# A two-layer trunk in split fp32: sums of normed tokens taken from PSUM, and VectorE's order around the MLP's seven-product multiplications

## The reference

```python
h2 = _rmsnorm(x, norm2_g[l])
x = x + jnp.square(jax.nn.relu(h2 @ w_ff1[l])) @ w_ff2[l]
```

## Time and profile before

| | |
|---|---|
| runs | 2473.15, 2473.32, 2476.62 us; median 2473.32 |
| profiled execution | 2465.62 us, its span 2463.8 us |
| granted TensorE clock, mean | 0.954 of full speed |
| busy, share of the span | TensorE 91%, VectorE 60%, GpSimd 43%, ScalarE 35% |
| first MLP | from about 502 to 1226 us of the span |
| second MLP | from about 1728 us to the end |

### The profile page before, as it was taken

One profiled execution on the slowest core, in us unless ns is written; L12 is line 12 of the kernel. 1 busy time (PEld: TensorE's weight loads), 2 busy tenths in 40 slices (PEclk: granted clock), 3 DMA queues, 4 the chain that ended last, 5 costly groups with the idle time before them and its releaser, 6 DMA issues.

```text
span 2463.8 us, 36690 instructions
## 1 busy us (share of the span) xinstructions
PE 2231.7 (91%) x12020; PEld 1875.0 (76%) x12020; DVE 1470.6 (60%) x1632; ACT 858.2 (35%) x1444; POOL 1065.7 (43%) x685
## 2 busy tenths in 40 slices
PE   7999979996999969999879999899959999699998
PEld 6988868884888757777679888788848877477776
DVE  4048753377888765565540587533778887656554
ACT  4133422244666621121142333321446665211210
POOL 4235322237556545353232453221375665453532
PEclk9999989998999989999989999799979999899999
DMA  7222233303777795656342231333137766966563
GB/s 256 83 66 85 87 107 93 125 34 130 240 246 251 243 375 214 247 201 252 123 136 82 69 98 68 109 112 104 57 118 247 248 241 230 378 228 232 218 241 128
DMA packets 225228, 418.93 MB, mean 170 GB/s; under 512 B 24664, under 2 KB 166616, under 8 KB 216800
## 3 DMA queue, kind: packets, MB, share of 16 engines
q1 hardware_dynamic: 209888, 394.47, 45.9%
q10 hardware_dynamic: 15232, 23.16, 2.6%
HBM read 264.40 MB, written 157.37 MB: 171 GB/s over the span
## 4 chain that ended last, share of the span: by engine, by line
PE 57%; issue 20%; POOL 9%; DVE 6%; SPq 4%; DMA 2%; ACT 1%; ACTq 0%; POOLq 0%; DVEq 0%
PE ps L1183 28%; PE ps L1493 19%; POOL w1s L1124 8%; SPq L476 2%; DVE xs L1961 2%; DVE tS L1947 1%; PE ps L1445 1%; POOL tT L1131 1%; PE ps L1278 1%; SPq L482 1%; PE ps L1174 1%; PE ps L1354 1%; PE ps L1348 1%; DMA raw<-in_wstream 1%; PE ps L1377 1%
## 5 line engine op out<-in xcount | busy, mean ns | idle before, releaser
L1493 PE MATMUL ps<-w2s,uk 128*128 128x512 f32 x2688 | 628.5, 395 | 76.9 <-DVE xs L1961 76.9
L1493 PEld LDWEIGHTS ps<-w2s,uk 128*128 128x128 f32 x2688 | 509.6, 191 | 195.7 <-DVE xs L1961 89.8
L1961 DVE TENSOR_TENSOR xs<-ps,xs 128x1024 f32<-128x1024 f32 x224 | 273.9, 1223 | 268.8 <-PE ps L1493 267.3
L1445 PE MATMUL ps<-hT,w1s 128*128 128x512 f32 x1344 | 322.9, 397 | 37.2 <-DVE uf L1920 25.9
L1445 PEld LDWEIGHTS ps<-hT,w1s 128*128 128x128 f32 x1344 | 258.2, 193 | 93.8 <-DVE uf L1920 26.7
L1135 POOL TENSOR_TENSOR w2s<-raw,w2s 128x1024 fp32r<-128x1024 f32 x64 | 172.6, 2699 | 326.6 <-ACT w2s L944 326.6
L1445 PE MATMUL ps<-tT,w1s 128*128 128x512 f32 x1008 | 251.6, 404 | 29.2 <-DVE uf L1929 17.8
L1445 PEld LDWEIGHTS ps<-tT,w1s 128*128 128x128 f32 x1008 | 193.3, 194 | 82.9 <-DVE uf L1929 30.0
L1124 POOL TENSOR_TENSOR w1s<-rawf,w1s 128x512 fp32r<-128x512 f32 x112 | 174.0, 1564 | 169.4 <-ACT w1s L849 169.4
L1183 PE MATMUL ps<-hT,whi 128*128 128x512 f32 x768 | 245.7, 401 | 0.0
L1183 PE MATMUL ps<-whi,hT 128*128 128x258 f32 x1280 | 239.0, 286 | 2.0 <-DVE hT L1539 1.4
(11 more groups left out here) (214 smaller groups left out, 3507.2 us busy)
## 6 DMA issues: line engine op xcount, KB each, us to landing
uk<-uD SPq DMA_DIRECT2D x64, 1024.0 KB, 7.0
raw<-in_wstream SPq DMA_DIRECT2D x104, 512.0 KB, 5.7
uk<-uD SPq DMA_DIRECT2D x64, 768.0 KB, 5.6
rawf<-in_wstream SPq DMA_DIRECT2D x64, 512.0 KB, 4.3
uD<-uh SPq DMA_DIRECT2D x64, 512.0 KB, 5.3
uD<-uf SPq DMA_DIRECT2D x64, 512.0 KB, 3.9
uD<-uh SPq DMA_DIRECT2D x64, 384.0 KB, 4.3
uD<-uf SPq DMA_DIRECT2D x64, 384.0 KB, 5.1
```

The source lines that it names most:

```text
L1445: mm = pe.matmul(ps[:, bank, :], w, x[:, k, :], start=(first and k == 0 and i == 0), stop=(k == 3 and i == 2), skip_group_check=True)
L1493: mm = pe.matmul(ps[:, bank + tp, :], u, w2s[r][:, w, k, :], start=(r in (1, 2, 5) and k == 0 and i == 0), stop=(k == 1 and i == 2), skip_ ...
L1961: V.tensor_tensor(y, ps[:, bank:bank + 2, :], y, ALU.add).then_inc(y_acc, 1)
```

## The change

The MLP of each layer is rearranged; the arithmetic of the products is the same, and no other stage is touched.

- In the norm loop ScalarE copies the first four tiles' two halves to SBUF as they are (`tf[1][:, 0]`, `b21`). For the last four tiles VectorE forms T1 and T2 directly from PSUM, tile by tile, with the scaling of a later tile between the two. T4 is then one full addition, and T3 is made from T2 in two. The seven full additions before the plain products' end and the three behind are gone (`t_step`).
- The low parts of T1, T2, T3 and T4 move from GpSimd (`sum_lo`) to VectorE (`t_lo_of`), and ScalarE's and VectorE's lists around them are in another order. T1 and T4 change places in SBUF.
- In each later chunk VectorE's second `u_los` goes behind the addition of product 7.
- In the last chunk product 4 comes before 7 and 3, into a bank of its own, with one more addition. SP's loads of residual tiles 4 and 5 wait for product 4 instead of 5.
- W2's sums are made one at a time, each behind an addition; in the first group the sums of the last hidden chunk also stand singly between additions.
- GpSimd's low parts of W2 are two instructions of 512 columns instead of one of 1024.

```diff
-        tT1 = at_x(16 * KB, "tT1", [P, 2, 4, 512], F32R)
-        tT4 = at_m(48 * KB, "tT4", [P, 2, 4, 512], F32R)
+        tT1 = at_m(48 * KB, "tT1", [P, 2, 4, 512], F32R)
+        tT4 = at_x(16 * KB, "tT4", [P, 2, 4, 512], F32R)
...
+        b21 = at_m(78 * KB, "b21", [P, 4, 512], F32)
...
-        ORD1, ORDZ = (1, 6, 5, 2, 7, 3, 4), (2, 1, 6, 5, 7, 3, 4)
+        ORD1, ORDZ = (1, 6, 5, 2, 7, 3, 4), (2, 1, 6, 5, 4, 7, 3)
...
-                sp.wait_ge(f_m, l * FM + FM - 7 + POSZ[5] + 1)
+                sp.wait_ge(f_m, l * FM + FM - 7 + POSZ[4] + 1)
                 alone(sp)
                 for t in (4, 5):
...
                 for t in range(NT):
+                    if t < 4:
+
+                        bank = (TB, OB)[t % 2]
+                        act.wait_ge(n_tr, nb * NT + (t + 1 + 2))
+                        nc.scalar.copy(tf[1][:, 0, :, t * P:(t + 1) * P], ps[:, bank, :].rearrange("p (k c) -> p k c", c=P)).then_inc(t_raw, 1)
+                        nc.scalar.copy(b21[:, :, t * P:(t + 1) * P], ps[:, bank + 1, :].rearrange("p (k c) -> p k c", c=P)).then_inc(t_raw, 1)
                     norm_hi(nb, t)
...
-                sum_hi(0, 1)
+                sum_hi(0, 1); sum_hi(1, 2)
                 for n, (a, hf) in enumerate(((0, 1), (1, 1))):
                     plain_hidden(0, n + 2, a, hf)
-                sum_hi(1, 2)
+                sum_hi(2, 4)
                 u_his(0, 0)
+                w1_hi(1, 0, 0)
                 plain_hidden(1, 0, 0, 1); plain_hidden(1, 1, 1, 1)
-                sum_hi(2, 4)
-                for pos in range(3):
+                w1_hi(1, 0, 1)
+                sum_hi(3, 3)
+                plain_hidden(1, 2, 0, 0)
+                for pos in (2, 3, 4):
                     w1_hi(1, 0, pos)
...
                 def w2_lo(g, r):
                     pool.wait_ge(m2_hi, l * (7 * GR) + (g * 7 + (POS2[r] + 1)))
-                    nc.gpsimd.tensor_tensor(w2s[r][:, 1], w2_from(r), w2s[r][:, 0].bitcast(F32), ALU.subtract).then_inc(m2_lo, 1)
+                    for k in range(2):
+                        e = nc.gpsimd.tensor_tensor(w2s[r][:, 1, k], w2_from(r)[:, k], w2s[r][:, 0, k].bitcast(F32), ALU.subtract)
+                    e.then_inc(m2_lo, 1)
...
-                sum_lo(0, 1); sum_lo(1, 2)
-                w1_lo(1, 0, 0); w1_lo(1, 0, 1); w1_lo(1, 0, 2)
-                sum_lo(2, 4)
-                sum_lo(3, 3)
-                for pos in range(3, 7):
+                for pos in range(7):
                     w1_lo(1, 0, pos)
...
-                norm_f(l)
                 nb = l * 2 + 1
-
-                def u_sums(j, c):
+                scale(nb, 0)
+                scale(nb, 1)
+                for t in range(NT):
+                    if t == 4:
+                        dve.wait_ge(s_spill, l * (32 * NT) + 32 * NT)
+                    if t >= 4:
+
+                        bank, c = (TB, OB)[t % 2], (t - 4) * P
+                        dve.wait_ge(t_raw, l * 8 + 2 * (t - 3))
+                        dve.wait_ge(n_hi, nb * NT + (t + 1))
+                        V.tensor_tensor(tf[1][:, 1, :, c:c + P], ps[:, bank, :].rearrange("p (k c) -> p k c", c=P), tf[1][:, 0, :, c:c + P], ALU.subtract).then_inc(t_sum, 1)
+                        if t + 2 < NT:
+                            scale(nb, t + 2)
+                        dve.wait_ge(t_sum, l * 11 + (2 * t - 7))
+                        V.tensor_tensor(tf[2][:, 1, :, c:c + P], ps[:, bank + 1, :].rearrange("p (k c) -> p k c", c=P), tf[1][:, 1, :, c:c + P], ALU.subtract).then_inc(t_sum, 1)
+                        norm_lo(nb, t)
+                    else:
+                        norm_lo(nb, t)
+                        scale(nb, t + 2)
...
-                dve.wait_ge(s_spill, l * (32 * NT) + 32 * NT)
-                dve.wait_ge(n_lo, nb * NT + NT + 2)
-                t_step(0, raw_of(1), H[12], H[11], SUB)
...
+                def t_lo_of(n, t):
+
+                    dve.wait_ge(t_hi, l * 4 + (n + 1))
+                    if t == 3:
+                        V.tensor_tensor(b_at_l[12], hTf[:, 1, 1, 0:4, :], b_at_h[12].bitcast(F32), SUB).then_inc(t_lo, 1)
+                    else:
+                        V.tensor_tensor(t_at[t][:, 1], tf[t][:, 1], t_at[t][:, 0].bitcast(F32), SUB).then_inc(t_lo, 1)
+
+
+                dve.wait_ge(t_sum, l * 11 + 8)
+                V.tensor_tensor(tf[4][:, 1], b21[:], tf[2][:, 1], SUB).then_inc(t_sum, 1)
+                t_lo_of(0, 1)
+                w1_sums(1, 0)
                 u_sums(0, 0)
                 u_los(0, 0, 0)
...
                 u_los(0, 0, 1)
-                w1_sums(1, 0)
                 dve.wait_ge(f_m, l * FM + 6)
...
+                V.tensor_tensor(hTf[:, 1, 1, 0:4, :], tf[2][:, 1], b_at_h[11].bitcast(F32), SUB).then_inc(t_sum, 1)
+                dve.wait_ge(t_sum, l * 11 + 10)
+                V.tensor_tensor(hTf[:, 1, 1, 0:4, :], hTf[:, 1, 1, 0:4, :], b_at_l[11].bitcast(F32), SUB).then_inc(t_sum, 1)
+                t_lo_of(1, 2)
+                t_lo_of(3, 3)
...
-                    u_los(jp, cp, 1)
                     dve.wait_ge(f_m, made(l, j, c, 7))
                     dve.wait_ge(f_w, added(l, j, c, 2))
                     V.tensor_tensor(u[:, A22, :], ps[:, o + 3, :], u[:, A22, :], ALU.add).then_inc(f_w, 1)
+                    u_los(jp, cp, 1)
...
+                def w2_sum(g, n):
...
+                    if n in (2, 3):
+                        dve.wait_ge(m2_sum, l * (4 * GR) + (g * 4 + (2 * n - 3)))
+                    out_, a, b = ((tS[0][:], b12, b11), (b12, b22, b12), (tS[1][:], b22, tS[0][:]), (tS[2][:], b21_, tS[1][:]))[n]
+                    V.tensor_tensor(out_, a, b, ALU.subtract).then_inc(m2_sum, 1)
...
-                w2_sums(0, 0)
                 u_los(LAST, 0, 1)
+                dve.wait_ge(f_m, FZ + POSZ[4] + 1)
+                V.tensor_tensor(u[:, 1, :], ps[:, 1, :], u[:, A12, :], ALU.add).then_inc(f_w, 1)
+                w2_sum(0, 0)
...
+                add(0, 0, 5, True)
+                for n, r in enumerate((6, 3, 7, 2)):
+                    u_sum_n(LAST, 1, n)
+                    add(0, 0, r, True)
...
                 def half_1(g, first, more):
...
+                    for n, r in enumerate(ORD2):
                         add(g, 1, r, first)
+                        if more and n in (0, 1, 3, 5):
+                            w2_sum(g + 1, (n + 1) // 2)
```

More of the change, by code:

```diff
@@ L277, in trunk_kernel @@
         m2_raw, m2_sum, m2_hi, m2_lo = [sem(f"m2_{n}") for n in ("raw", "sum", "hi", "lo")]
-        t_sum, t_hi, t_lo = [sem(f"t_{n}") for n in ("sum", "hi", "lo")]
+        t_raw, t_sum, t_hi, t_lo = [sem(f"t_{n}") for n in ("raw", "sum", "hi", "lo")]
         f_m, f_m1, f_w, f_rel, f_sq, y_m, y_acc = [sem(n) for n in ("f_m", "f_m1", "f_w", "f_rel", "f_sq", "y_m", "y_acc")]
@@ L947, in _ @@
                 FZ = l * FM + FM - 7
-                AZ = l * FW + FW - 6
+                AZ = l * FW + FW - 7
                 hidden(LAST, 0, 3, A12, None, f_w, added(l, LAST, 0, 5))
@@ L955, in _ @@
                 w2_hi(0, 5, f_m, FZ + POSZ[5] + 1)
[L956 to L961, removed]
+                hidden(LAST, 1, 1, A22, None, f_w, AZ + 5)
+                w2_hi(0, 6, f_m, FZ + POSZ[7] + 1)
+                w2_hi(0, 3, f_m, FZ + POSZ[7] + 1)
+                hidden(LAST, 1, 2, A21, None, f_w, AZ + 6)
+                w2_hi(0, 7, f_m, FZ + POSZ[7] + 1)
+                hidden(LAST, 1, 3, A12, None, f_w, AZ + 7)
                 w2_hi(0, 2, f_m, FZ + POSZ[3] + 1)
@@ L1466, in _ @@
                 pe.wait_ge(f_rel, l * (4 * CH) + 4 * (CH - 2) + 1)
-                for r, bank, first in ((2, 0, True), (1, 4, True), (6, 5, True), (5, 6, True), (7, 7, True), (3, 6, False), (4, 7, False)):
+                for r, bank, first in ((2, 0, True), (1, 4, True), (6, 5, True), (5, 6, True), (4, 1, True), (7, 7, True), (3, 6, False)):
                     pe.wait_ge(m1_lo, made(l, LAST, 1, r))
-                    if r in (3, 4):
-                        pe.wait_ge(f_w, l * FW + FW - 6 + {3: 3, 4: 4}[r])
+                    if r == 3:
+                        pe.wait_ge(f_w, l * FW + FW - 7 + 3)
                     product_1(r, bank, first, True)
@@ L1540, in norm_lo @@
                                 hT[:, t // 4, 0, :, (t % 4) * P:(t % 4) * P + P].bitcast(F32), ALU.subtract).then_inc(n_lo, 1)
-            def norm_f(l):
-                nb = l * 2 + 1
-                scale(nb, 0)
-                scale(nb, 1)
-                for t in range(NT):
-                    norm_lo(nb, t)
-                    if t + 2 < NT:
-                        scale(nb, t + 2)
             with dve.Fori(0, DEPTH) as l:
@@ L1842, in u_sums, with u_sum_n @@
+                SUB = ALU.subtract
+                def u_sum_n(j, c, i):
                     n = l * (4 * CH) + (j * 8 + 4 * c)
                     u = uf[c % 2]
-                    if isinstance(j, int) and j == 0:
+                    if i == 0:
```

(23 more changed lines are left out.)

81 lines of the change are left out of this document (15 added, 66 removed).

## The result

The changed kernel takes 2393.18 us (median of four runs, 2389.05 to 2394.07), the kernel before 2473.24 beside it: a ratio of 0.9672, 95% interval 0.9655 to 0.9688. My forecast was 2356 with a range to 2388: the direction held, the size did not, by 37 us. The profiled execution took 2393.15 (span 2391.4); before it was 2465.62, so 72.5 less, where the sum said 117.

The account below looks back on a forecast made before the run. TensorE, busy 91% of the span, was taken as the bound, its stops nearly all in the MLP. Gains 43.6 + 15.5 + 52 + 6 = 117 off 2465.62 gave 2348.5, plus 7.7 for the median: 2356, range 2336 to 2388.

Parts of the forecast that it names:

- W2's sums: Second MLP product, steady groups: one sum per addition removes both TensorE stops, 43.6 us in all, bounds 22 and 43.6.
- The first rival: Steady groups: W2's sums go on holding up additions, one of two stops stays, 2378 us; chance 0.14.
- The turn: Start of second MLP product: stop of 9.74 goes, mostly waited away at the W2 load; 6 us, bounds 0 and 10.
- The change of phase: Plain products to seven-product pairs: 30.3 got back less 4.2 lost in the norm loop, 26 a layer, 52 in all.
- VectorE's order in the pairs: Seven-product pairs: u_los moved behind the addition the last product waits for, 15.5 us gained, bounds 8 and 18.
- The 0.1 a pair: Pairs: allowance left after judging the moved u_los's effect on the next addition and SP's store of that low part.
- The difference of the median and the profile: Whole kernel: median of the runs lies 7.7 us above the profiled execution, added to 2348.5 to forecast 2356.
- The second: Rival: VectorE becomes the bound at the change of phase, 10 a layer instead of 26, 2388 us; chance 0.12.
- the five: Rivals: sums still block, VectorE bound, shorter turn queue, later W2 loads, stops unchanged; chances 0.14, 0.12, 0.07, 0.03, 0.02.

Follow-up runs that it names:

- e5: The kernel before with only W2's sums made one per addition, GpSimd's low parts left whole: 2420.46 us, ratio 0.9792.
- e6: The changed kernel with GpSimd's low parts of W2 whole again instead of in halves: 2392.83 us, ratio 0.9683.
- e8: The changed kernel with SP's second load of W2 issued ahead of the last chunk's stores: 2380.70 us, ratio 0.9635.
- e3: The changed kernel with VectorE's second u_los one place further on, behind the addition of product 3: 2394.56 us, ratio 0.9697.
- e11: The changed kernel with SP's stores of the hidden sums held until the W1 load ahead of them has landed: 2374.09 us, ratio 0.9609.
- e12: e9 plus, in the norm loop's tiles 4 and 5, the scaling of a later tile ahead of the first sum from PSUM: 2334.31 us, ratio 0.9450.
- e9: The changed kernel with a second buffer for a row of W1 and the second W2 load ahead of the stores: 2337.05 us, ratio 0.9460.
- e4: The changed kernel with a second buffer for one row of W1's raw tile in every other chunk: 2349.08 us, ratio 0.9512.

## Why the prediction missed, step by step

- **W2's sums: right.** 43.6 forecast for the steady groups; TensorE's two stops a group are gone, a group takes 38.08 for 41.71, and e5 shows that this edit alone gives the whole gain of the second phase. The first rival, a stop that stays, did not come, and with whole low parts it did not come either (e6).
- **The turn: right in size.** 50.1 less 43.6 leaves 6.5 for a forecast of 6. That most of the gain from the first stop would be waited away at the W2 load is what e5 shows; e8 shows that SP's order holds a third of the stop at that load.
- **The change of phase: 47.7 of 52.** The part behind the loop came out as listed: 29.6 and 30.3 got back in the two layers, where I had 30.3 (stops of 0.63 and 1.21 where I had 0.9 and 0.7). The loop lost 6.7 in layer 0 and 5.5 in layer 1, and not 4.2. Its stops are 2.07 and 0.88, as worked out (2.2, 0.9), and the transposes of the third tile came 2.70 late for y where the loop before waits 1.48, as the two ScalarE copies have no cover. What I left out: behind the stop of 2.07 the 24 multiplications took 4.64 for 3.12. The windows of that stretch (length; busy time of TensorE, its weight loads, VectorE, ScalarE and GpSimd; then the granted clock, the DMA share and GB/s):

```profile
530.60:531.60 1.00, 0.95 (x8) 0.95 (x9) 0.97 (x2) 0.00 (x0) 0.91 (x1) 1.00 0.00 0
531.60:532.60 1.00, 1.00 (x7) 1.00 (x6) 1.00 (x2) 0.00 (x0) 0.00 (x0) 0.52 0.00 0
532.60:533.60 1.00, 1.00 (x7) 1.00 (x6) 0.45 (x1) 0.00 (x0) 0.00 (x0) 0.50 0.00 0
533.60:534.60 1.00, 1.00 (x7) 1.00 (x6) 0.00 (x0) 0.00 (x0) 0.00 (x0) 0.50 0.00 0
534.60:535.60 1.00, 1.00 (x9) 1.00 (x9) 0.00 (x0) 0.00 (x0) 0.00 (x0) 0.77 0.00 0
```

  The clock falls to 0.50, the lower level of 1.2 GHz, soon after the stop, for some 3 us: 1.5 us a layer beside the stop itself.
- **VectorE's order in the pairs: the step that failed.** I forecast 15.5 us of gain, with bounds of 8 and 18; it cost 25.5 in that stage. I read that product 4 waits for the addition of 7, that u_los stands ahead of that addition, and took the wait to vanish with u_los. But W1's sums stand ahead of both, and they waited for their load in the kernel before as well (the waits of layer 0's twelve pairs have 10.0 us of it); the load waits for GpSimd's last low part, and that for the sums of the pair before. I followed a wait back one step, where it had to be followed until it came round to itself. So with these links a pair could not be shorter than the ring, 19.47, however VectorE's list was ordered: 24 pairs of it are 467.3, so of the 474.9 at most 7.6 was to be had. What the move did was to let the additions behind it, and with them the four hidden sums, start earlier in the ring: 5.40 after W1's fourth sum (672.77 less 667.37), where they started 6.54 after it (729.35 less 722.81). So the hidden sums now run beside more of GpSimd's two raw parts behind each other (2.56 became 3.00, the whole of what took the parts from 10.52 to 10.96). The stores of the high parts that ScalarE makes of these sums go out a little earlier in the ring, and the load, behind the longer parts, later, so the stores stand closer behind it (4.92 became 5.53). That is 1.07 a pair, 25.7 in 24 pairs, for 25.5 measured. u_los grew too (2.28 to 2.92), but in e3 it did not and the parts were as long; that it is the hidden sums which lengthen the raw parts is read from the rows of five kernels, and no run moves them alone. The 0.1 a pair that I had left for side effects has neither link in it: I had looked at the store of the low part alone, and at no load behind which stores are issued. The Trainium skill ("SBUF — State Buffer", section "Who interferes with whom") says that VectorE's instructions with two SBUF inputs and GpSimd's that read SBUF take turns. The trace agrees (u_los 2.28 became 2.92, two raw parts 2.56 became 3.00). I had weighed this rule for W2's sums and for the change of phase, and not for the pairs.
- **The difference of the median and the profile.** I added 7.7 for the profiled execution being quicker than the median. After the change the two agree (2393.15 and 2393.18), so this hid as much of the error: by profiles the miss is 2348.5 against 2393.15, 44.6, of which the pairs are 41.0 and the change of phase 4.3.
- **The rivals.** The second, VectorE as the bound at the change of phase, named the nearest time (2388) for a thing that did not happen. None of the five had the pairs in it; I had given that step bounds of one sign.

## What to carry to other kernels

When an instruction waits, follow the wait back until it ends in something that does not depend on the instruction itself; if it comes round (here load, sums, low parts, load, through one buffer), the sum of the ring is the floor, and only an edit to a link of it, or a second buffer, helps. Add up that ring before pricing a change of order: a move that takes nothing out of it can at best leave its links as they are, and here it lengthened two. An edit that moves an instruction beside another engine's work needs a lower bound below nothing.

## What the runs showed of the hardware that I had not expected

- A load of 1 MB followed on the same queue by 1.75 MB of stores 1.4 us later lands at 5.5 us, and at 4.6 to 4.7 when the stores wait for it (e11, medians): what is issued behind a load delays it.
- The norm loop's stop of TensorE of 2.05 to 2.07 stands in both layers of the changed kernel and of the seven runs made from it that keep this loop (all but e12), sixteen times. Behind thirteen of them the 24 multiplications took 4.6 at a granted clock of about 0.5 (1.2 GHz), behind one 4.27 (e9, layer 0), and behind two 3.12 to 3.14 at 1.00 (layer 0 of e4 and e6), for the same length of stop within 0.03. Behind e12's stops of 0.57 the clock held in both layers. What decides is not shown.
